# Modulation rows of the later layers: partial products on VectorE, one summing matmul pair on TensorE

## What is computed

```
cs = jax.nn.silu(c)
for l in range(DEPTH):
    mod = cs @ w_mod[l] + b_mod[l]                         # (B, 3D)
    shift, scale, gate = jnp.split(mod[:, None, :], 3, axis=-1)
    h = rmsnorm(x, g_pre[l]) * (1 + scale) + shift
    y = mla_band_mixer(h, ...) or spatial_gating_mixer(h, ...)
    x = x + gate * rmsnorm(y, g_post[l])
```

## Time and profile before

| | us |
|---|---|
| median of 3 runs (4477.6, 4511.96, 5175.38) | 4511.96 |
| the profiled execution | 4480.95 |
| its span on the slowest core, core 1 | 4479.3 |
| spans of the 8 cores | 4441.2 to 4479.3 |
| TensorE busy | 4330.8 (97%) |
| VectorE busy | 1621.8 (36%) |
| ScalarE busy | 1319.6 (29%) |
| GpSimd busy | 474.1 (11%) |

### The profile page before, as it was taken

One profiled execution on the slowest core, in us unless ns is written; L12 is line 12 of the kernel. 1 busy time (PEld: TensorE's weight loads), 2 busy tenths in 40 slices (PEclk: granted clock), 3 DMA queues, 4 the chain that ended last, 5 costly groups with the idle time before them and its releaser, 6 DMA issues.

```text
span 4479.3 us, 74816 instructions; the slowest of 8 cores (4441.2 to 4479.3 us)
## 1 busy us (share of the span) xinstructions
PE 4330.8 (97%) x28028; PEld 2424.7 (54%) x28028; DVE 1621.8 (36%) x3255; ACT 1319.6 (29%) x2427; POOL 474.1 (11%) x465
## 2 busy tenths in 40 slices
PE   4788999999999999999999999999999999999999
PEld 1456767676544444444445677766664444444444
DVE  1552222333366244111565332233336724411133
ACT  1535553222232132000333556322223313200011
POOL 1221100000000002222001101000000000222200
PEclk8899999999999999999999999999999999999999
DMA  9938663543966887657756667464376576633743
GB/s 178 186 57 100 103 89 56 80 51 42 170 196 163 182 195 162 92 81 101 221 185 103 88 106 95 59 79 59 40 123 208 177 158 164 140 59 57 113 158 141
DMA packets 570395, 539.33 MB, mean 120 GB/s; under 512 B 327311, under 2 KB 501647, under 8 KB 546359
## 3 DMA queue, kind: packets, MB, share of 16 engines
q0 software_dynamic: 293216, 239.09, 38.4%
q1 hardware_dynamic: 276826, 295.45, 22.9%
HBM read 617.72 MB, written 100.78 MB: 160 GB/s over the span
## 4 chain that ended last, share of the span: by engine, by line
PE 92%; DMA 4%; issue 1%; DVE 1%; ACT 1%; POOL 1%; another core or an unknown queue 0%; SPq 0%; DVEq 0%; ACTq 0%; POOLq 0%
PE PS L290 87%; PE PS L288 5%; DMA W<-w_mod 1%; DMA RG<-w_mod 1%; DMA RG<-sg_w_out 1%; POOL W L312 0%; ACT R L300 0%; DVE RG L309 0%; DMA W<-ab_w_in 0%; PE PS L1510 0%; DMA acc<-EYE 0%; DMA EYE<-acc 0%; ACT W L300 0%; SPq L327 0%
## 5 line engine op out<-in xcount | busy, mean ns | idle before, releaser
L300 ACT ACTIVATE R<-PS 128x512 bf16<-128x512 f32 (+4 forms) x1760 | 894.1, 527 | 2325.9 <-PE PS L290 1573.9
L290 PE MATMUL PS<-W,RG 128*128 128x256 bf16 (+3 forms) x10368 | 1497.8, 295 | 14.5 <-DMA W<-ab_w_in 13.9
L290 PE MATMUL PS<-RG,W 128*128 128x512 bf16 x6528 | 1490.2, 379 | 0.0
L290 PEld LDWEIGHTS PS<-W,RG 128*128 128x128 bf16 x10368 | 957.2, 98 | 508.2 <-issue 41.8
L290 PE MATMUL PS<-RG 128*128 128x512 bf16 x4320 | 1010.3, 376 | 10.6 <-DMA RG<-RG 6.8
L290 PEld LDWEIGHTS PS<-RG,W 128*128 128x128 bf16 x6528 | 631.1, 98 | 715.0 <-issue 21.5
L290 PEld LDWEIGHTS PS<-RG 128*128 128x128 bf16 x4320 | 423.1, 98 | 475.3 <-issue 15.9
L312 DVE TENSOR_TENSOR RG<-PS,R 128x512 bf16<-128x512 f32 (+1 forms) x192 | 129.0, 689 | 725.3 <-PE PS L290 725.2
L300 ACT ACTIVATE RG<-PS 128x2048 bf16<-128x2048 f32 (+2 forms) x127 | 161.3, 1283 | 674.6 <-PE PS L290 668.6
L288 PE MATMUL PS<-R 128*128 128x129 bf16 (+2 forms) x2928 | 341.1, 226 | 13.6 <-issue 9.9
L290 PE MATMUL PS<-R 128*128 128x128 bf16 (+3 forms) x1332 | 306.3, 289 | 5.6 <-ACT R L300 5.2
(11 more groups left out here) (94 smaller groups left out, 2055.5 us busy)
## 6 DMA issues: line engine op xcount, KB each, us to landing
W<-w_mod POOLq DMA_DIRECT2D x64, 1024.0 KB, 10.0
W<-ab_w_in POOLq DMA_DIRECT2D x80, 512.0 KB, 8.7
RG<-w_mod POOLq DMA_DIRECT2D x32, 1024.0 KB, 17.0
VR<-R SPq DMA_DIRECT2D x128, 256.0 KB, 8.1
R<-VR SPq DMA_DIRECT2D x32, 1024.0 KB, 7.8
W<-sg_w_in POOLq DMA_DIRECT2D x32, 1024.0 KB, 13.3
XB<-R SPq DMA_DIRECT2D x20, 1024.0 KB, 3.8
R<-XB SPq DMA_DIRECT2D x20, 1024.0 KB, 5.5
```

What stands on the lines that cost most here:

```text
L290: P.op("pe", lambda e: e.matmul(o, lhsT, rhs, start=start, stop=stop), r=r, w=w, sig=sig)
L300: P.op("act", lambda e: e.activation(out=o, in_=i, func=func, **kw), r=r, w=w, wp=wp)
```

## The change

A step now loads 512 columns of 1024 contraction rows (`cgrp_load`; the same 1 MB). VectorE multiplies each of its eight 128 x 512 strips by the matching column of silu(c), one value per partition, and adds it to `acc` in float32 (`cgrp_mac`). After two steps `acc` holds, on each partition, that partition's share of 512 output columns. The bias is added on partition 0, `cgrp_split` writes the sum as two bfloat16 halves (high part and remainder), and TensorE adds up the 128 partitions with two matmuls against a matrix of ones (`cgrp_sum`). VectorE finishes one partition of the bank with the norm weight, and 512 columns go to DRAM. The 80 steps remain; there are 40 sums.

In the attention layers a list `sched` holds every single strip, load, split and sum with a due job; `poll` takes them off in order, and stops at a sum while a projection group is open. In the gMLP layers `per` changes, the steps of a pass move a little later, and a sum is issued two tiles (passes 0 to 3) or one unit (passes 4 to 11) after its second step. Pass 0 of layer 1 now has two steps, pass 4 none.

```diff
-        def mod_mm(l, k, s, buf, toks, b, gtile, gtoks, early=False):
...
-            for q in range(2):
-                kc = 2 * s + q
-                for j in range(4):
-                    mm(bank(b)[32 * j:32 * j + 32, :], csrep[:, kc:kc + 1].to_broadcast([128, 32]), bv[:, q, j * 512:(j + 1) * 512], q == 0, q == 1,
...
-                tt("dve", acc[:], acc[:], bank(b), ALU.add, r=[PS_t[b], acc_t], w=[acc_t])
...
+        def cgrp_load(l, k, s, buf, toks):
+
+            j, h = s // 2, s % 2
+            wload(buf.rearrange("p (k c) -> p k c", c=512), w_mod[l, h * 1024:(h + 1) * 1024, k * 2048 + j * 512:k * 2048 + (j + 1) * 512], toks)
+
+        def cgrp_mac(s, q, buf, toks, fresh):
+
+            kc = 8 * (s % 2) + q
+            wv = buf[:, q * 512:(q + 1) * 512]
+            if fresh and kc == 0:
+                ts("dve", acc[:], wv, ccol_t[:, 0:1], None, ALU.mult, None, r=toks + [c_t], w=[acc_t])
             else:
...
+                stt("dve", acc[:], wv, ccol_t[:, kc:kc + 1], acc[:], ALU.mult, ALU.add, r=toks + [c_t, acc_t], w=[acc_t])
...
+        def cgrp_split(hl, hlt):
+            cp("dve", hl[:, 0:512], acc[:], r=[acc_t], w=hlt)
+            tt("dve", hl[:, 512:1024], acc[:], hl[:, 0:512], ALU.subtract, r=[acc_t] + hlt, w=hlt)
+
+        def cgrp_sum(l, k, s, hl, hlt, b, row, rowt):
+
+            j = s // 2
+            for x in range(2):
+                mm(bank(b), ones1[:, 0:1].to_broadcast([128, 128]), hl[:, x * 512:(x + 1) * 512], x == 0, x == 1, r=hlt + [c_t], w=[PS_t[b]], sig=(x == 1))
...
+            dma("sp", MODROW[l, k, j * 512:(j + 1) * 512].unsqueeze(0), o, r=rowt, wp=[MR_t[l][k]])
...
+                while sched and sched[0][0] <= at:
+                    if sched[0][2] and fb["busy"] is not None:
                         return
...
+                    sched.pop(0)[1]()
...
-            per = [0, 2, 2, 2, 3, 3, 3, 3, 3, 2, 1, 0] if len(mods) == 24 else [0, 0, 0, 0, 2, 1, 1, 1, 1, 1, 1, 0]
+            per = [2, 2, 2, 2, 0, 2, 3, 3, 3, 3, 2, 0] if len(mods) == 24 else [0, 0, 0, 0, 0, 0, 2, 2, 2, 2, 0, 0]
...
+                hl, hlt = (buf[:, 0:1024], toks) if p == 3 else (Rb(26, 2), RT(26, 2))
+                cgrp_split(hl, hlt)
+                late_.append((at, lambda: cgrp_sum(l_, w_, s_, hl, hlt, nb(), GT_, GTt)))
...
+                if p == 0 or not nm and p < 11:
+                    next_weights(p)
                 for k in range(min(nm, 2)):
                     m_load(p)
...
+                    while late_ and late_[0][0] <= s:
+                        late_.pop(0)[1]()
+                    if todo and s >= ((9, 10) if p == 0 else (5, 6) if p < 4 else (3, 4) if p == 5 else (2, 3, 4))[nm - todo]:
+                        m_mac(p, s + (2 if p < 4 else 1))
                         if nm == 3 and todo == 3:
                             m_load(p)
```

More of the change, by code:

```diff
@@ L933, in even_layer @@
             cur = [-1]
+            GT_, GTt = Wf(30, 2), WT(30, 2)
+            base = [40 * n for n in range(8)] + [320 + 28 * n for n in range(9)]
+            sched = []
             def mbuf(k):
@@ L962, in head_tiles @@
+            plan_mods()
             def head_tiles(n, g):
@@ L1063, in poll @@
             def poll(n, hj):
-                if fb["busy"] is not None:
-                    return
-                if 0 < n < 6 and n_a:
-                    if min(n_a, ((n - 1) * 40 + hj) * n_a // 190) > mstate["mm"]:
-                        m_mm()
-                        if mstate["load"] < n_a:
-                            m_load()
-                elif len(mq) and 7 <= n <= 10:
-                    per = n_b // 4
-                    done = mstate["mm"] - n_a - per * (n - 7)
-                    if done >= per:
-                        return
-                    slot = n_head[n] // per
-                    if mstate["load"] == mstate["mm"]:
-                        if hj >= done * slot:
-                            m_load()
-                    elif hj >= done * slot + slot - 2:
-                        m_mm()
+                at = base[n] + hj
+                while sched and sched[0][0] <= at:
+                    if sched[0][2] and fb["busy"] is not None:
+                        return
+                    sched.pop(0)[1]()
             tail, qr_mm, qr_done = todo
@@ L1140, in even_layer @@
                         if n == 1:
-                            for _ in range(min(2, n_a)):
-                                m_load()
+                            for k in range(min(2, n_a)):
+                                m_load(k)
                         fl = plan(n)
@@ L1358, in odd_layer @@
                         todo -= 1
-                        if todo == 0 and p < 11:
+                    if wait_w and not todo and not (late_ and p == 3):
+                        wait_w = False
+                        if p < 11:
                             next_weights(p)
@@ L1400, in odd_layer @@
                             state["mix"] += 1
-                while todo:
-                    m_mm()
-                    todo -= 1
-                    if todo == 0 and p < 11:
-                        next_weights(p)
+                assert not todo and not late_ and not wait_w
         def startup():
```

121 lines of the change are left out of this document (77 added, 44 removed).

## The result

The changed kernel is slower: the ratio to the kernel before is 1.039, with a 95% interval of 1.035 to 1.043. The profiled execution took 4657.9 us where the one before took 4480.95: +177 us. The prediction had +113.5.

The account below looks back on a forecast made before the run. TensorE was taken to bound the kernel (92% of the chain). Waits 113 + clock 24 + attention 25 + sums 17 - steps 51 - old waits and clock 14.5 = +113.5 us on 4480.95: 4594 us, range 4455 to 4680.

Parts of the forecast that it names:

- passes 6 to 10 and layer 3: Late gMLP passes: sums wait 5.8 us in each of passes 6 to 9, 3.9 in the others; 43 us.
- the split's 2.4 us: VectorE before each sum: bias, high part and remainder one behind another take 0.86 + 0.86 + 0.69 us.
- Waits at the sums: gMLP layers: TensorE waits for VectorE at the sums, 33 + 26.5 + 10.5 + 43 = 113 us.
- Pass 0: Layer 1: two loads land 30.2 and 34.5 us after issue, so TensorE waits 33 us at the sum.
- Clock: TensorE behind some 15 waits of over 2.3 us: lower clock costs 24 us, from 0 to 42.
- What goes: gMLP layers: old waits before steps, 10.1 us, and lower clock behind them vanish, together 14.5 us.
- Attention: Attention layers: strips bunch up on VectorE and hold up outputs and projections; 25 us lost, bounds 0 and 70.
- the steps' 0.64 us: TensorE's old steps: each costs 0.64 us, so 80 of them going saves 51 us.
- the pitch: VectorE's strips: 0.69 us plus 0.17 us, so 0.86 us from strip to strip, 6.9 us for eight.
- The first rival: VectorE strips at two columns a cycle, 0.6 us apart; waits together 61.5 us, total time 4512 us; chance 0.20.
- The second rival: No sum waits long, needing pass 0's loads to land 30 us earlier; -49 us, 4432 us; chance 0.06.
- The third: Attention is VectorE's: TensorE loses 70 us and more there behind runs of strips; 4660 us; chance 0.14.

Follow-up runs that it names:

- the run above: Changed kernel with GpSimd's multiply of a unit moved to VectorE from pass 6 on; mean span 4605.2 us, 14 less than the changed kernel.
- The idle matmuls: Changed kernel in which TensorE runs matmuls whose result is overwritten ahead of each gMLP sum; mean span 4592.4 us, 27 less than the changed kernel.
- The bank counter run: Changed kernel with the counter that hands out the banks moved on by 4 at the end of layer 1; mean span 4607.8 us, 12 less.
- Without strips: Changed kernel leaving out all attention strips but the first of each group; attention 905.6 us in layer 0 and 895.2 in layer 2, 27 less together.
- the attention-only run: New scheme in the attention layers alone, gMLP layers as in the kernel before; mean span 4464.2 us, where the kernel before had 4460.4.
- the two accumulators: Changed kernel summing odd strips of passes 1 and 2 into a second tile, added at the end; mean span 4612.6 us, 7 less.
- the run with them first: Changed kernel issuing pass 0's two strip loads ahead of the next weights instead of behind them; mean span 4610.4 us, pass 0 10.7 us less.

## Why the prediction was right and wrong

The direction and the mechanism hold: TensorE waits at the sums for VectorE, and runs at the lower clock behind the waits. The time does not: +152 us by the stages, where the sum had +113.5. The step that failed is the sizing of the waits in passes 6 to 10 and layer 3, by the split's 2.4 us; the 38.6 us that are missing come from it and from smaller terms.

**Waits at the sums: 113 predicted, 131.7 measured on core 1.** Passes 1 and 2: 8.0 for 7.5 and 7.9. Pass 3: 10.5 for 9.7. Pass 5: 10.5 for 11.7. So far the chains counted out are right to about 1 us. Passes 6 to 10 and layer 3: 43 for 58.3, and this is the largest part of the miss. In the trace pass 6 waits 6.7 us, pass 7 4.8 and 3.8, pass 8 6.8, pass 9 4.7 and 4.4, pass 10 and each of layer 3's four 5.4: about 1.4 us more at every one of eleven sums. The step that failed is "bias, high part, remainder behind one another: 0.86 + 0.86 + 0.69 = 2.4 us", which took the split's rows from instructions beside which GpSimd did nothing. Beside GpSimd's multiply and load issue, high part and remainder take 1.2 and 1.45 us (in the run above: 1.1 and 0.69, and 0.8 us less wait). In pass 6 strips, too, run for 7.44 us instead of 6.72:

```profile
1870.31 0.69 DVE L313 TENSOR_TENSOR RG<-PS,R 128x512 bf16<-128x512 f32 x1 [2.79 <-POOL R L313]
1870.92 7.44 DVE L310 SCALAR_TENSOR_TENSOR acc<-W,ccol_t,acc 128x512 f32<-128x512 bf16 x8
```

Pass 0: 33 for 36.6. The prediction took "they landed 30.2 and 34.5 us later" as the time of these loads, and on core 1 they now took 33.9 and 39.3. But 30.2 and 34.5 were one core's: before, on six cores, the two took 28.0 to 36.0 and 34.5 to 42.6 us, and now 31.3 to 34.9 and 37.2 to 41.1. So core 1 had been early, and the range should have been some 8 us wide. That the smaller pieces of 512 columns slow the loads is not shown; the means differ by 1.3 and 0.5 us, less than the cores do among each other. The sentence "even in the crowd of pass 0 no load took more than 34.5 us" was true of that core alone.

**Clock: 24 predicted (0 to 42), 31 to 32 measured.** The idle matmuls gave 31.1 us back, and the count in the trace is 31.8. The number of waits was right, 15 for 16; the price was not. I had taken the smaller of two stretches, 1.6 us, and each wait cost 2 us.

**What goes: 14.5 predicted, 9.1 measured.** The 10.1 us of old waits and 4.4 us of old clock are core 1's, the slowest core before. On the mean of cores 1, 2 and 3 all waits of the gMLP layers were 9.3 us and the clock 2.6, and 2.8 us of other waits stand in the changed kernel. With this the gMLP layers add up: 131.0 of waits at the sums (mean of the three cores), 16 sums 6.9, clock 31.8, less 32 steps 20.5, less 9.1, are 140.1 of the 141.6 us by which they grew.

**Boundary 1 and the low rank part behind it: 0 predicted, 6.3 measured.** This was not in the sum at all. The bank counter run shows that it is the number of calls to the bank allocator: 7.1 us of the boundary go with it.

**Attention: 25 predicted, 24 by the table, 33 without the stray wait.** 48 steps at 0.64 us went (30.7) and 24 sums at 0.433 came (10.4), so with no loss these stages should be 20.3 us shorter. They are 3.3 longer: 23.6 us lost. But the kernel before had its stray wait there; against its cores without it, layer 0 grew by 8 us, and the loss is 33. Without strips 27 come back. That the term looks exact is luck in part. The expectation of the attention-only run put the forecast at 12 us more in each stage and so forgot the 20.3; by the forecast's own terms it is +5 in both together, and +3.5 was measured there.

The rest is right: the steps' 0.64 us, the sums' 0.2165 us a matmul, and, by two errors that cancel, the pitch. A strip lasts 0.75 us and the next begins 0.104 us behind it, 0.855 together where I had added 0.69 and 0.17 to 0.86. The first rival falls with that: a strip takes 0.75 us and not the 0.42 of its rate of two columns a cycle. (Its waits also add up to 61.1 us and not to 61.5, which changes nothing.) The rule of the Trainium skill on which it leaned ("Vector Engine (DVE) Microarchitecture Reference", section on points easy to get wrong) halves the rate with two SBUF sources that are not bfloat16, which left room for a full rate with one that is; here the form with one bfloat16 source takes 0.75 us, no less than the 0.69 of two float32 sources. The other rule that was weighed, of the Trainium skill ("VectorE: DVE Perf Modes", section on the DRAIN), would have the next strip start without a cost for its dependence; the two accumulators show 0.19 us of cost. The second rival needed the loads of pass 0 to land 30 us earlier; in the run with them first they landed 32 us earlier, and 23.8 us of wait were left. The third, 70 us in attention at 4660 us in all, lies near the measured 4657.9 by chance: its cause is refuted by the 27 us of all its strips. Of the 4657.9, 25 us are core 7's attention of layer 0 and no term of the sum.

## What to carry to other kernels

When a job moves from the busiest engine to an idle one, price the hand-back first: here most of the 500 us of added VectorE work was hidden, and yet the 34 us saved on TensorE (51 less 17) were lost four times over (132 us) where it stood at a result that was not ready. Put the consumer several tiles behind its producer, and then look again, since under a wait there may be others: banks behind the same queue, a buffer that is held longer, a store queue. Take the durations of a chain from rows in which the other engines do what they will do beside it, and the landing of a load from all cores and not from one. Add to each wait of TensorE what the clock takes behind it.

## What the runs showed of the hardware

- SCALAR_TENSOR_TENSOR of a bfloat16 strip, a scalar from a pointer and a float32 tile, 512 columns: 0.75 us. Dependent ones follow every 0.855 us, independent ones every 0.66 us.
- TENSOR_SCALAR of the same strip to float32: 0.47 us. An operation on one partition of 512 columns takes 0.68 us, as much as on 128.
- Behind the waits at the sums TensorE's granted clock stood at 1.2 GHz, for 63.6 us outside the waits in all; with matmuls in the waits it stayed at 2.4 GHz throughout the gMLP layers, and the mean span was 27 us shorter.
- VectorE's instructions get longer beside GpSimd's multiply: a remainder of the split 0.69 and 1.45 us, strips 0.75 and, for the 18 that overlap it, 1.14 in the mean. A CAST took 0.43 us alone and 1.12 beside a load issue of GpSimd's, in the row above; that the issue is the cause is not shown.
- Two loads of 1 MB behind the same weight load, issued at the same point of pass 0 on six cores, took 28.0 to 36.0 us and 34.5 to 42.6 us to land. A forecast from one core's time has that scatter in it.
